# Two stretches of a decoder trunk rearranged: the first norm, and the low-rank inputs of the second layer

## The reference, cut to what matters

```
def rmsnorm(x, g, eps=RMS_EPS):
    y = xf * lax.rsqrt(jnp.mean(xf * xf, axis=-1, keepdims=True) + eps)
    return y * g

# even layer
xn = rmsnorm(h, norm_mix[0]);  u = xn @ w_in

# odd layer
xn = rmsnorm(h, norm_mix[1])
x_prev = concat([x_last, xn[:, :-1]])
xmix = xn + (x_prev - xn) * mu            # six mixtures: r, w, k, v, a, g
r = xr @ w_r;  k = xk @ w_k;  v = xv @ w_v
log_w = -exp(-softplus(-(w0 + tanh(xw @ w1) @ w2)) - 0.5)
a = sigmoid(a0 + (xa @ a1) @ a2)
```

## Time and profile before

| what | us |
|---|---|
| median of three executions | 1999.93 |
| the profiled execution, its own time | 1991.22 |
| its span from first to last instruction | 1989.4 |
| PE busy in it | 1775.6 |
| DVE busy | 1054.4 |
| ACT busy | 768.2 |
| mean granted TensorE clock | 0.932 of full speed |

### The profile page before, as it was taken

The page is one execution under the profiler, slowest core; times in us unless marked ns, Lnnn a source line. Parts: engine busy times, 40 slices in busy tenths (PEclk is TensorE's granted clock), DMA queues, the critical chain, the costliest instruction groups (busy, mean ns, idle before and its releaser), DMA issues.

```text
span 1989.4 us, 42983 instructions
## 1 busy us (share of the span) xinstructions
PE 1775.6 (89%) x18597; PEld 1665.3 (84%) x18597; DVE 1054.4 (53%) x1518; ACT 768.2 (39%) x1019; POOL 128.7 (6%) x152
## 2 busy tenths in 40 slices
PE   3999978899999999976898967767899999999997
PEld 3999876799999999974886856766389999999997
DVE  5377775644434444448588556652654443444444
ACT  3253454355412223332255335542445441222234
POOL 1042451000000000000000000001110000000000
PEclk8999999899999999988899958887799999999999
DMA  3221231332332233230121210001043332223321
GB/s 103 75 75 55 54 94 54 86 117 84 93 98 64 85 97 93 69 96 1 54 75 54 68 32 4 4 14 35 0 95 113 88 104 84 73 85 93 90 72 57
DMA packets 237228, 138.50 MB, mean 70 GB/s; under 512 B 6576, under 2 KB 232304, under 8 KB 237088
## 3 DMA queue, kind: packets, MB, share of 16 engines
q1 hardware_dynamic: 226528, 114.31, 20.2%
q0 software_dynamic: 4048, 13.67, 2.7%
q10 hardware_dynamic: 6512, 8.42, 1.4%
HBM read 128.22 MB, written 8.16 MB: 69 GB/s over the span
## 4 chain that ended last, share of the span: by engine, by line
PE 78%; DVE 12%; ACT 5%; issue 2%; POOL 1%; DMA 1%; ACTq 0%; DVEq 0%; POOLq 0%
PE ps L340 63%; PE ps L2178 1%; PE ps L1510 1%; PE ps L2172 1%; PE ps L1785 1%; PE ps L975 1%; DVE w_rest L309 1%; ACT w_head L304 1%; DVE x_split L1836 1%; PE ps L2187 1%; PE ps L1051 1%; DMA mix<-in_x_sample 1%; DVE mix L1770 1%; PE ps L2454 1%; ACT mix L2277 0%
## 5 line engine op out<-in xcount | busy, mean ns | idle before, releaser
L340 PE MATMUL ps<-x_split,w_head 128*128 128x272 f32 (+1 forms) x5568 | 945.3, 292 | 50.1 <-DVE x_split L1836 21.2
L340 PEld LDWEIGHTS ps<-x_split,w_head 128*128 128x128 f32 x5568 | 799.8, 191 | 71.4 <-issue 49.0
L340 PE MATMUL ps<-x_split,w_rest 128*128 128x272 f32 (+1 forms) x2784 | 582.3, 291 | 0.0
L304 ACT ACTIVATE w_head<-w_raw 128x1024 fp32r<-128x1024 f32 (+1 forms) x206 | 228.3, 1108 | 602.6 <-PE ps L340 591.7
L340 PEld LDWEIGHTS ps<-x_split,w_rest 128*128 128x128 f32 x2784 | 441.8, 192 | 0.0
L309 DVE TENSOR_TENSOR w_rest<-w_raw,w_head 128x1024 fp32r<-128x1024 f32 (+1 forms) x206 | 268.3, 1303 | 190.3 <-ACT w_head L304 190.3
L340 PE MATMUL ps<-hidden_split,w_head 128*128 128x272 f32 x1408 | 233.2, 287 | 0.0
L340 PEld LDWEIGHTS ps<-hidden_split,w_head 128*128 128x128 f32 x1408 | 198.0, 188 | 0.0
L340 PE MATMUL ps<-hidden_split,w_rest 128*128 128x272 f32 x704 | 145.3, 287 | 0.0
L1341 DVE TENSOR_TENSOR hT<-hT,ps 128x544 f32<-128x544 f32 (+1 forms) x40 | 28.9, 721 | 161.6 <-PE ps L340 161.6
L340 PEld LDWEIGHTS ps<-hidden_split,w_rest 128*128 128x128 f32 x704 | 110.1, 188 | 0.0
(11 more groups left out here) (427 smaller groups left out, 2010.4 us busy)
## 6 DMA issues: line engine op xcount, KB each, us to landing
w_raw<-in_w_ffn_gate SPq DMA_DIRECT2D x44, 512.0 KB, 3.8
...
```

The source lines that it names most:

```text
L304: act.activation(wh[:, s, 0:kt * P], raw[:, s, 0:kt * P], ACT.Copy).then_inc(head_ok[s], 1)
L340: mm = pe.matmul(ps[:, 2 * s + h, 0:half.stop - half.start], w[:, s, k * P:(k + 1) * P], x[:, k, half], start=first and k == 0, stop=k == ...
```

## The change

**The start.** SP now issues the input, as five DMAs with a semaphore each, then the two weight slabs of `f_b`, then the constants and small vectors. ACT issues the identity and the gain of the first norm, spread over all partitions. As token tile tt arrives, PE transposes it as before (DVE copies it to `hT`) and ACT squares it in token rows with a sum over the row (`accum_out`). Ln and Exp run on 5 columns. The tiles are scaled by rstd and gain still in token rows: 0, 2, 4 by DVE, 1 and 3 by POOL and ACT. PE transposes the scaled tokens, ACT and DVE split straight from PSUM. The first unit of `f_b` is in two halves, k 0 to 3 inside the second row of transposes, and k 4 to 7 behind it. The small vectors are transposed behind the first unit.

**The odd layer.** POOL issues the six loads (as 12 DMAs) when the feed-forward part of the first layer has ended, and multiplies w1 and a1 by their mu on the partitions. Since (xn + dx mu) w1 = xn w1 + dx (mu w1), PE makes both low-rank inputs from `xn` and `dx` at once, w in 64 columns and a in the other 64, with no mixtures made. DVE makes norm, difference, mixture r and its rest tile by tile, and PE takes the low-rank products of tile q together with the tiles of the first two units of `rw_r`. The 8 output tiles of w and a are put inside units 2, 3 and 4, and the decay sums behind them; the factor -exp(-0.5) moves into the scale of later activations.

```diff
+        ytk = cols(5 * D + 2 * P, 5, D)
+        mix_gain = cols(10 * D + 2 * P, D)
+        token_rs = cols(11 * D + 2 * P, 8)
...
+        groups = [(half, tt) for half in range(2) for tt in range(5)]
+
+        def sp_x(sp):
+            for tt in range(4):
+                sp.dma_start(xtok[:, tt, :], a["x_prompt"][0, tt * P:(tt + 1) * P, :]).then_inc(x_in[tt], 16)
+            sp.dma_start(xtok[0:TS, 4, :], a["x_sample"].rearrange("b t d -> (b t) d")).then_inc(x_in[4], 16)
...
+            act.dma_start(mix_gain, a["norm_mix"][0].partition_broadcast(P)).then_inc(gain_in, 16)
+            for tt in range(5):
+                act.wait_ge(x_in[tt], 16)
+                n = rows_of(tt)
+                act.activation(ytk[0:n, tt, :], xtok[0:n, tt, :], ACT.Square, accum_out=token_rs[0:n, tt:tt + 1]).then_inc(
+                    *E0.act.done(f"sq{tt}"))
+            act.wait_ge(*E0.act.at("sq4"))
+            act.wait_ge(*E0.dve.at("eps"))
+            pieces = ((slice(0, P), slice(0, 4)), (slice(0, TS), slice(4, 5)))
+            for rows, at in pieces:
+                act.activation(token_rs[rows, at], token_rs[rows, at], ACT.Ln, bias=eps[rows, 0:1],
+                               scale=1.0 / D).then_inc(*E0.act.done(f"ln{at.start}"))
+            act.wait_ge(*E0.act.at("ln4"))
+            for rows, at in pieces:
+                act.activation(token_rs[rows, at], token_rs[rows, at], ACT.Exp, scale=-0.5).then_inc(
+                    *E0.act.done(f"rstd{at.start}"))
+            act.wait_ge(*E0.act.at("rstd4"))
+            for tt in (1, 3):
+                act.wait_ge(*E0.pool.at(f"xg{tt}"))
+                act.activation(ytk[:, tt, :], ytk[:, tt, :], ACT.Copy, scale=token_rs[:, tt:tt + 1]).then_inc(
+                    *E0.act.done(f"y{tt}"))
+            act_head(act, "f_b", 0, 0)
+            for g, (half, tt) in enumerate(groups):
+                n = rows_of(tt)
+                act.wait_ge(*E0.pe.at(f"y{g}"))
+                act.activation(xh[:, 4 * half:4 * half + 4, tt * P:tt * P + n],
+                               ps[:, 4 + g % 4, 0:4 * n].rearrange("p (k t) -> p k t", k=4), ACT.Copy).then_inc(
+                    *E0.act.done(f"h{g}"))
+                if g == 4:
+                    act_head(act, "f_b", 1, 0)
...
+        def pool_embed(pool):
+            pool.wait_ge(gain_in, 16)
+            for tt in (1, 3):
+                pool.wait_ge(*E0.act.at(f"sq{tt}"))
+                pool.tensor_tensor(ytk[:, tt, :], xtok[:, tt, :], mix_gain, ALU.mult).then_inc(*E0.pool.done(f"xg{tt}"))
...
+                if half == 0:
+                    pe.wait_ge(*(E0.act if tt in (1, 3) else E0.dve).at(f"y{tt}"))
+                if g >= 4:
+                    pe.wait_ge(*E0.dve.at(f"l{g - 4}"))
+                to_features(pe, ytk, 4 + g % 4, half, tt).then_inc(*E0.pe.done(f"y{g}"))
+                if g == 6:
+                    pe.wait_ge(head_ok[0], 1)
+                    pe.wait_ge(rest_ok[0], 1)
+                    pe.wait_ge(*E0.dve.at("l4"))
+                    for k in range(4):
+                        first_products(pe, k)
+            pe.wait_ge(*E0.dve.at("l9"))
+            for k in range(4, KT):
+                mm = first_products(pe, k)
+            mm.then_inc(mm_ok[0], 1)
...
+            for tt in (0, 2, 4):
+                n = rows_of(tt)
+                dve.scalar_tensor_tensor(out=ytk[0:n, tt, :], in0=xtok[0:n, tt, :], scalar=token_rs[0:n, tt:tt + 1],
+                                         in1=mix_gain[0:n, :], op0=ALU.mult, op1=ALU.mult).then_inc(*E0.dve.done(f"y{tt}"))
+            dve_rest(dve, "f_b", 0, 0)
+            for g, (half, tt) in enumerate(groups):
+                n = rows_of(tt)
+                at = (slice(0, P), slice(4 * half, 4 * half + 4), slice(tt * P, tt * P + n))
+                dve.wait_ge(*E0.act.at(f"h{g}"))
+                dve.tensor_tensor(xl[at], ps[:, 4 + g % 4, 0:4 * n].rearrange("p (k t) -> p k t", k=4), xh[at].bitcast(F32),
+                                  ALU.subtract).then_inc(*E0.dve.done(f"l{g}"))
+            dve_rest(dve, "f_b", 1, 0)
...
-        def act_mix(act):
-            act.wait_ge(added_ok, 9)
+        def pool_low(pool):
+
             for i in range(2):
-                act.wait_ge(mm_ok[i], used["rw_r"][i])
-            act.dma_start(tab[:, 0:1064], a["odd_tables"]).then_inc(*O0.dma.loaded("tab"))
-            act.dma_start(odd_levels[:, :], a["odd_levels"]).then_inc(*O0.dma.loaded("levels"))
-            act.dma_start(w1, a["rw_w1"][0].rearrange("(k p) n -> p k n", p=P)).then_inc(*O0.dma.loaded("w1"))
-            act.dma_start(a1, a["rw_a1"][0].rearrange("(k p) n -> p k n", p=P)).then_inc(*O0.dma.loaded("a1"))
-            act.dma_start(w2, a["rw_w2"][0]).then_inc(*O0.dma.loaded("w2"))
-            act.dma_start(a2, a["rw_a2"][0]).then_inc(*O0.dma.loaded("all"))
...
+            pool.wait_ge(*O0.dma.at("all"))
+            for k in range(KT):
+                for m, at in ((0, 1), (1, 4)):
+                    side = slice(64 * m, 64 * m + 64)
+                    pool.tensor_scalar(down_dx[k][:, side], down_x[k][:, side], col("rw_mu", 8 * at + k), None,
+                                       ALU.mult).then_inc(*O0.pool.done(f"down{k}{m}"))
+
+        low_tiles = {2: ((2, 0), (4, 1), (6, 2)), 3: ((1, 3), (3, 4), (5, 5)), 4: ((1, 6), (4, 7))}
...
+            for q in range(KT + 4):
+                if q < KT:
+                    pe.wait_ge(*O0.dve.at(f"dx{q}"))
+                    for w, x in ((down_x, xn), (down_dx, dx)):
+                        for h in range(2):
+                            mm = pe.matmul(ps[:, 4 + h, 0:TH], w[q], x[:, q, h * TH:(h + 1) * TH],
+                                           start=q == 0 and w is down_x, stop=q == KT - 1 and w is down_dx)
+                    if q == KT - 1:
+                        mm.then_inc(*O0.pe.done("low"))
+                if 1 <= q < KT + 1:
+                    pe.wait_ge(*O1.dve.at(f"rw_rl{q - 1}"))
+                for s, k in ((0, q - 1), (1, q - 4)):
+                    if 0 <= k < KT:
+                        mm = tile_products(pe, "rw_r", s, k)
+                        if k == KT - 1:
+                            mm.then_inc(mm_ok[s], 1)
+            for u in range(2, KT):
+                unit_products(pe, "rw_r", u // 2, u % 2, low_rank(u), u == KT - 1)
...
+                        for b, r, name in ((4, slice(0, 64), "w2"), (6, slice(64, P), "a2")):
+                            if i > 0:
+                                pe.wait_ge(*O0.act.at(f"{name[0]}{i - 1}"))
+                            elif name == "a2":
+                                pe.wait_ge(*O0.dve.at("shift"))
+                            for h in range(2):
+                                mm = pe.matmul(ps[:, b + h, 0:TH], low2[i // 3][r, i % 3 * P:(i % 3 + 1) * P],
+                                               low[r, h * TH:(h + 1) * TH], start=True, stop=True)
+                            mm.then_inc(*O0.pe.done(f"{name}{i}"))
+
...
+                if u == 0:
+                    act.wait_ge(*O0.pe.at("low"))
+                    act.activation(two(low[0:64, :]), ps[0:64, 4:6, 0:TH], ACT.Tanh).then_inc(*O0.act.done("lw"))
+                    act.activation(two(low[64:P, :]), ps[64:P, 4:6, 0:TH], ACT.Copy).then_inc(*O0.act.done("la"))
+                for _, k in low_tiles.get(u + 1, ()):
+                    act.wait_ge(*O0.pe.at(f"w2{k}"))
+                    if k >= 4:
+                        act.wait_ge(*O1.dve.at(f"mid{k - 4}"))
+                    act.activation(two(t_of(k)), ps[:, 4:6, 0:TH], ACT.Sigmoid, bias=col("rw_w0", k)).then_inc(
+                        *O0.act.done(f"w{k}"))
+                    act.wait_ge(*O0.pe.at(f"a2{k}"))
+                    act.activation(two(a_of(k)), ps[:, 6:8, 0:TH], ACT.Sigmoid, bias=col("rw_a0", k)).then_inc(
+                        *O0.act.done(f"a{k}"))
...
+        def dve_r(dve):
+            dve.wait_ge(*norm_o.s.act.at("rstd"))
+            normal(dve, 0)
             for k in range(KT):
-                for k in range(KT):
-                for k in range(KT):
+                if k + 1 < KT:
+                    normal(dve, k + 1)
+                shifted(dve, k)
+                if k > 0:
+                    x_rest(dve, "rw_r", k - 1)
+                dve.wait_ge(*O0.dve.at(f"dx{k}"))
+                mixed(dve, "rw_r", k)
+            x_rest(dve, "rw_r", KT - 1)
...
+                    dve.tensor_copy(lioS, ps[0:72, 7, 0:P]).then_inc(*O0.dve.done("shift"))
+                for _, k in low_tiles.get(u, ()):
+                    decay_sums(dve, k)
+
+        def decay_sums(dve, k):
+
+            dve.wait_ge(*O0.act.at(f"w{k}"))
+            dve.tensor_tensor_scan(qrF[:, k, 1, :], resetO, t_of(k), 0.0, ALU.mult, ALU.add).then_inc(*O0.dve.done(f"b{k}"))
+            dve.wait_ge(*O0.dve.at(f"b{k}"))
+            dve.tensor_tensor(qrF[:, k, 0, :], qrF[:, k, 1, :], t_of(k), ALU.subtract)
```

(6 more changed lines are left out.)

310 lines of the change are left out of this document (150 added, 160 removed).

## The result

The changed kernel takes **1945.7 us** (median of 4 runs, 1943.0 to 1946.5) beside 2001.0 for the kernel before (median of 4): the ratio is 0.971, 95% interval 0.966 to 0.976. It is clearly faster, and 10 us faster than the 1956 that I had given. Its profiled execution took 1946.39 us with a span of 1944.2, against 1991.22 and 1989.4. With all executions of this study together the medians are 1996.7 (82 executions, 1988.8 to 2017.8) and 1946.5 (16, 1941.7 to 1955.7), 50.2 us apart. Ratios and medians of the experiments leave out executions more than 1.5% above the fastest of their kernel (one of e2, two of e11).

What follows compares the result with a forecast made beforehand. TensorE, busy 89% of the span, was taken as the bound, so gains come where it stands or runs cold. -12.6 - 30.2 - 0.8 = -43.6 took 1991.22 to 1947.6; 8.7 from profile to median gave 1956 us, range 1943 to 1970.

Steps and rivals of the forecast that it cites:

- (d): Odd layer, units 2 to 7 of `rw_r` with the low-rank output products: 52.4 us, `rw_r` ending at 972.7 against 1002.9.
- stall: Odd layer, in (d): the first product with a2 waits 1.4 us for DVE's copy of the shift rows.
- Start: From the input's arrival to the second unit, which begins at 36.0 instead of 48.6: -12.6 us.
- cold start: Rival, at the start: the clock stays at 1.2 GHz through transposes and first unit, +8 to +11 us; chance 0.12.
- (a): Odd layer's norm: DMA issues moved to POOL and the table loaded early let Ln start at 886.4, -3.2 us.
- (b): Odd layer, DVE's round per tile (norm, difference, small ones, rest and mixture): 3.1 us, first difference ready at 891.5.
- (c): Odd layer, PE's low-rank products with units 0 and 1: 26.7 us plus 1.8 for half clock, done at 920.3.
- (e): At `rw_k`, DVE no longer has 0.8 us of mid sums before it mixes: -0.8 us.
- Odd place in all: Odd layer to the end of `rw_r`, which comes at 972.7 against 1002.9: -30.2 us, the -3.2 of (a) included.
- DVE and ACT: Rival, odd layer: thin covers in units 2 to 7 give way, eight output tiles stall, +11 us, 1967; chance 0.12.
- the slow clock: Rival, mixed stretch of `rw_r`: the clock falls to half, +15.9 us net if throughout, 2016 us; chance 0.04.
- More than forecast: Rival: tokens land at 10, no stall, low-rank output products overlap, perhaps no clock fall at the start: 1948 us; chance 0.10.

Runs made afterwards that it cites:

- e2: The kernel before with the new start alone, its old odd layer kept; ratio 0.990 to the kernel before.
- e11: The changed kernel with unread transposes in both gaps of the start and the shift rows' transpose and copy moved ahead; ratio 0.967 to the kernel before, median 1936.2 us.
- e5: The changed kernel with 24 unread transposes between those of the raw and the scaled tokens; ratio 0.972 to the kernel before.
- e12: The kernel before with only its six loads of low-rank weights issued by POOL instead of ACT; ratio 0.9974 to the kernel before.
- e7: The changed kernel with the low-rank output products of a in the same rows as those of w; ratio 0.979 to the kernel before.
- e1: The kernel before once more, unchanged; ratio 1.000 to the kernel before.
- e14: The kernel before, unchanged, executed again for its trace; 2004.1 us.
- e18: e11 with 24 more unread transposes behind the odd layer's sum of squares; ratio 0.974 to the kernel before, median 1941.9 us.

## Why the prediction was wrong

The forecast was 1956, the changed kernel takes 1946. The mechanisms in the sum were those described, with the overlap that it left out: both places gave their terms or more, the slower rivals didn't come. **The step that failed is the term for the low-rank output products in (d)**, "again 64 x 0.23 = 14.7": it is too large. With its stall it stood at 16.1 and measured 11.1, since products in different rows of the array overlap. Means of the four traces of before and the three of the changed kernel, place by place:

- *Start*, forecast -12.6: measured -13.7 at the first unit's end, of which 1.0 is given back in the gap at 59 (34.8 to 35.8). The steps: last tile landed at 11.5 (12.0, forecast), its squares from 11.94, rstd at 16.5 (17.2), transposes at 17.93 (18.6), the rest of the first unit at 31.46 (32.5), second unit at 34.71 (36.0). The cold start came (row below), and cost nothing that shows, since DVE set the pace (e5): the 1.6 that I had put in for it wasn't due, and the rival's 8 to 11 neither. Stretch of the changed kernel:

```profile
17.90:24.00 6.10, 5.54 (x27) 0.50 0.24 61
```

- *(a)*, forecast -3.2: -3.1 (e12). *(b)*, forecast 3.1 us a round: 2.87. *(c)*, both first units done at 920.3, which is 907.9 with the 12.4 that the start had moved that place: 908.3.
- *(d)*, from there to the end of `rw_r`, forecast 52.4: 956.7 - 908.3 = 48.4. The output products took 2.40 + 6 x 1.19 + 1.59 = 11.1 us with their stall, where I had 14.7 + 1.4. e7 shows why: in the same rows a tile is 2.10, in different rows 1.19. I had weighed this very rule (the Trainium skill, TensorE: Matmul & The Clock Gate, Part 3: Packing small matmuls) at 1.8 us for all eight tiles, counting one overlapped record in each, and left it out of the sum. The trace agrees with the rule, and it is worth 5 to 6. I had taken 0.23 from products that all lay in the same rows, and so from the wrong row. Against that stands 0.8 us that I had not: the tile of `rw_r` behind each group took 0.86 us instead of 0.75, eight times.
- *(e)*, forecast -0.8: -0.8 (161.83 to 161.02 in the table).
- *Odd place in all*, forecast -30.2: -33.6 profile against profile, -35.5 by the means. The difference between these two is that the one execution of before which I had was quicker there than its three sisters by 2 us: its clock was back when the low-rank products began. The stretch from 908 on, in that trace and in e1:

```profile
908.00:916.00 8.00, 8.00 (x33) 0.98 0.01 2
```

```profile
908.00:916.00 8.00, 8.00 (x27) 0.79 0.01 2
```

Over all columns the difference of the means is -49.9, where I had -43.6. The start's surplus and what the gap at 59 gave back cancel. Of the 6.3 us, 3.4 are the odd place between the two profiles (4.0 in (d)), 1.9 the quick first trace, and 1.0 the even layer, where one of the four traces of before (e14) took 3.5 more. That it looked right at first, -44.8 between the two profiled executions, was a draw: the first trace of before lay 5 us under the mean of its four. The other thing was the base. I added the 8.7 us between the profiled execution and the median of three, and that median (1999.93) lies 3.2 above that of 82 executions. So 1956.3 - 3.2 - 6.3 = 1946.8: the product term is the step of the sum that failed, and the base weighs about as much.

Two readings of the prediction were wrong and cost little. It took a group of four transposes as 0.8 us at full clock and 1.6 at half, from 6.59 for 40. The profile gives 1.00 for that stretch, but the first 22 took 0.21 us each, as those at a granted 0.50 did in the changed kernel, and the full ones behind them 0.11: a group is 0.43 us at the quick pace and 0.86 at the slow one. The 1.00 at 12.80 was therefore no sign against a cold start. And 891.5 with 26.7 and 1.8 is 920.0, not 920.3.

The rival *DVE and ACT* didn't come: TensorE was busy 55.46 of 55.50 us between 884.5 and 940. Nor did the slow clock, which was 1.00 there; the only half clock in the odd place is around and behind the norm, at a price of 0.5 to 2.2 us (e18). *More than forecast*, with a chance of 0.10, came: of its terms the overlap was there in triple, the stall wasn't avoided (that took e11), and the tokens landed at 11.5, not 10. That the time came near its 1948 is partly luck, since the base did as much for it as the overlap.
